# A two-layer hybrid encoder step: weight slots, token remainders and the last hidden tile around the seven-product MLP

## What is computed

```python
def _residual(x, mix, p):
    x = x + _rmsnorm(mix, p['g_post_mix'])
    f = jnp.square(jax.nn.relu(_rmsnorm(x, p['g_pre_mlp']) @ p['w_ff1'])) @ p['w_ff2']
    return x + _rmsnorm(f, p['g_post_mlp'])
```

## Time and profile before

| | |
|---|---|
| median of 3 runs | 2267.86 us (2266.67 to 2268.46) |
| the profiled execution | 2269.92 us, its span 2268.2 us |
| PE busy | 2207.9 us (97%) |
| PEld busy | 2109.3 us (93%) |
| DVE / ACT / POOL busy | 1165.3 / 1025.0 / 1022.9 us |
| chain that ended last | PE 86%, DVE 7%, ACT 3%, issue 2% |
| granted TensorE clock, mean | 0.995 |

### The profile page before, as it was taken

The page is one execution under the profiler, slowest core; times in us unless marked ns, Lnnn a source line. Parts: engine busy times, 40 slices in busy tenths (PEclk is TensorE's granted clock), DMA queues, the critical chain, the costliest instruction groups (busy, mean ns, idle before and its releaser), DMA issues.

```text
span 2268.2 us, 40754 instructions
## 1 busy us (share of the span) xinstructions
PE 2207.9 (97%) x16722; PEld 2109.3 (93%) x16722; DVE 1165.3 (51%) x2353; ACT 1025.0 (45%) x1939; POOL 1022.9 (45%) x788
## 2 busy tenths in 40 slices
PE   7999999999999999999999999999999999999997
PEld 7999988899999999999989999888999999999997
DVE  5677555535415315666576765455353261256654
ACT  4454433434555642334444544444355565324332
POOL 2423324435564463646423332244356635545642
PEclk9999999999999999999999999999999999999999
DMA  5122221122124122222321223111212422222221
GB/s 191 64 74 73 93 73 56 57 74 66 66 85 171 54 87 93 85 82 78 112 81 54 83 82 94 57 57 58 78 57 75 158 80 75 84 84 94 92 86 51
DMA packets 64569, 187.85 MB, mean 83 GB/s; under 512 B 8800, under 2 KB 17824, under 8 KB 63744
## 3 DMA queue, kind: packets, MB, share of 16 engines
q1 hardware_dynamic: 56160, 169.28, 22.2%
q10 hardware_dynamic: 8224, 15.97, 1.9%
HBM read 170.99 MB, written 10.89 MB: 80 GB/s over the span
## 4 chain that ended last, share of the span: by engine, by line
PE 86%; DVE 7%; ACT 3%; issue 2%; POOL 1%; DMA 1%; SPq 0%; DVEq 0%; ACTq 0%; POOLq 0%
PE dense L1037 39%; PE att L1037 23%; PE att L1061 4%; PE dense L1061 3%; PE att L1395 1%; PE att L1305 1%; PE dense L1117 1%; PE att L1325 1%; PE att L1162 1%; DVE h_raw L2211 1%; PE att L1353 1%; PE att L1244 1%; PE att L1240 1%; PE att L1470 1%; POOL wlo L2622 1%
## 5 line engine op out<-in xcount | busy, mean ns | idle before, releaser
L2622 POOL TENSOR_TENSOR wlo<-wraw,whi 128x1024 fp32r<-128x1024 f32 x245 | 604.4, 2481 | 491.1 <-ACT whi L1532 491.1
L1037 PE MATMUL dense<-h_hi,whi 128*128 128x280 f32 x1712 | 506.3, 296 | 4.2 <-DVE ckv L2105 1.5
L1037 PE MATMUL dense<-h_lo,whi 128*128 128x280 f32 x1712 | 499.3, 292 | 0.0
L1037 PE MATMUL dense<-h_hi,wlo 128*128 128x280 f32 x1712 | 498.1, 291 | 0.0
L1532 ACT ACTIVATE whi<-wraw 128x1024 fp32r<-128x1024 f32 x302 | 310.3, 1049 | 115.9 <-DMA wraw<-in_w 110.2
L1037 PEld LDWEIGHTS dense<-h_hi,whi 128*128 128x128 f32 x1712 | 321.9, 188 | 16.4 <-issue 9.7
L1037 PEld LDWEIGHTS dense<-h_hi,wlo 128*128 128x128 f32 x1712 | 321.4, 188 | 0.7
L1037 PEld LDWEIGHTS dense<-h_lo,whi 128*128 128x128 f32 x1712 | 321.7, 188 | 0.0
L1037 PE MATMUL att<-hid_hi,whi 128*128 128x280 f32 x704 | 209.4, 297 | 15.7 <-DVE facc L2129 6.6
L2627 POOL TENSOR_TENSOR hid_lo<-hid_raw,hid_hi 128x560 fp32r<-128x560 f32 (+1 forms) x76 | 96.2, 1271 | 257.7 <-ACT hid_hi L1557 186.4
L1037 PE MATMUL att<-hid_hi,wlo 128*128 128x280 f32 x704 | 207.1, 294 | 0.0
(11 more groups left out here) (482 smaller groups left out, 5467.4 us busy)
## 6 DMA issues: line engine op xcount, KB each, us to landing
wraw<-in_w SPq DMA_DIRECT2D x266, 512.0 KB, 3.5
wraw<-in_w SPq DMA_DIRECT2D x72, 256.0 KB, 3.5
x_spill<-x ACTq DMA_DIRECT2D x2, 2240.0 KB, 6.9
x<-x_spill ACTq DMA_DIRECT2D x2, 2240.0 KB, 12.2
k_cat<-k_rope SPq DMA_DIRECT2D x16, 212.0 KB, 3.4
x<-in_x SPq DMA_DIRECT2D x4, 560.0 KB, 7.3
out_y_out<-x SPq DMA_DIRECT2D x4, 560.0 KB, 3.1
out_c_out<-ckv SPq DMA_DIRECT2D x2, 560.0 KB, 5.5
```

The costliest lines, as they stand in the source:

```text
L1037: mm = pe.matmul(bank(u, o, hf)[0:m, :], keys, b[:, k, H[hf]], start=(k == 0 and i == 0), stop=(k == kt - 1 and i == 2))
L2622: pool.tensor_tensor(wlo[slot][:, :], wraw[slot][:, :], whi[slot][:, :].bitcast(F32), ALU.subtract).then_inc(pool_done, st.done("pool", f" ...
```

## The change

- `slots_for`: the weights of the first pair (16, 17) may not use slot `SUMS`, and "ff2 27" may not use `EDGE[3]`. By the planner's rule "ff1 even 16" goes to slot 1, "ff1 odd 16" to slot 2, "ff2 two 12" to `SUMS`, "ff2 27" to slot 2 and "ff2 28" to `EDGE[3]`.
- `w_hi`: ScalarE rounds the even tile of a pair ahead of the pair's three sums instead of behind them.
- `token_sums` on VectorE: the remainders of token sums 0, 2 and 1 come after "ff2 two" 8, 9 and 10; before, 0 and 2 came after 8 and 1 after 9.
- hidden tile 31 is activated, rounded and subtracted in two halves, far tokens first, and "ff2 two 28" runs both output tiles over the far tokens and then over the near ones.

```diff
--- before.py
+++ after.py
@@ -707,12 +707,12 @@
             def slots_for(l, u):
                 kind, n = KINDS[u]
                 if kind.startswith("ff1 ") or kind == "ff2 two":
-                    return [*BASE, *MLP] if kind == "ff2 two" and n < 12 else [*BASE, *MLP, SUMS]
+                    return [*BASE, *MLP] if (kind == "ff2 two" and n < 12) or (kind != "ff2 two" and n == STRASSEN[0]) else [*BASE, *MLP, SUMS]
                 if kind in ("out", "ff1", "ff2"):
                     if kind == "out" or (kind == "ff1" and n < 8):
                         return [*MLP, *MIX] if u in U_MIX else [*BASE, *MIX] if u in V_MLP else [*BASE] if kind == "out" else [*BASE, *MLP]
                     if kind == "ff2" and n >= 24:
-                        return [*MLP, *BASE] if u == U_MLP[0] else [*MLP, *BASE, EDGE[3]] if u in U_MLP else [*BASE]
+                        return [*MLP, *BASE] if u in U_MLP[0:2] else [*MLP, *BASE, EDGE[3]] if u in U_MLP else [*BASE]
                     return [*BASE, *MLP]
                 return [*EDGE, *BASE] if u < LAP + 2 else [*BASE]
 
@@ -1018,6 +1018,20 @@
                                     mm.then_inc(pe_done, st.done("pe", f"half {u} 0 {hf}"))
                         st.mark("pe", f"dense {u}")
                         return
+                    if (kind, n) == ("ff2 two", LAST_TWO[1]):
+                        for hf, end in ((1, " far"), (0, "")):
+                            for o in range(nout):
+                                wait_bank(u, o, hf)
+                                for k in range(kt):
+                                    if o == 0 and (hf == 1 or k == kt - 1):
+                                        for e, name in ready_names(kind, n, k):
+                                            pe.wait_ge(by_name[e], A(e, name + (end if k == kt - 1 else "")))
+                                    for i, (a, b) in enumerate(((hi_w, hi_x), (lo_w, hi_x), (hi_w, lo_x))):
+                                        mm = pe.matmul(bank(u, o, hf), a[:, o, k, :], b[:, k, H[hf]],
+                                                       start=(k == 0 and i == 0), stop=(k == kt - 1 and i == 2))
+                                mm.then_inc(pe_done, st.done("pe", f"half {u} {o} {hf}"))
+                        st.mark("pe", f"dense {u}")
+                        return
                     for o in range(nout):
                         for hf in hfs:
                             wait_bank(u, o, hf)
@@ -1519,7 +1533,12 @@
                 count = {"stored": 0}
 
                 def w_hi(u):
+                    if KINDS[u][0] == "ff1 even":
+                        return
                     if KINDS[u][0] == "ff1 sums":
+                        even = slot_of[l, u - 2]
+                        act.wait_ge(w_loaded[even], loads[l, u - 2])
+                        act.activation(whi[even][:, :], wraw[even][:, :], ACT.Copy).then_inc(act_done, st.done("act", f"w hi {u - 2}"))
                         for i, (raw, _, hi) in enumerate(sums):
                             act.wait_ge(dve_done, A("dve", f"sum {i} {u}"))
                             act.activation(hi, raw, ACT.Copy).then_inc(act_done, st.done("act", f"w hi {u} {i}"))
@@ -1535,6 +1554,14 @@
                 def strassen(u):
                     for i, parts in enumerate(((f"early early {u}", f"evac {u} 0 1"), (f"late late {u}", f"evac {u} 1 0"))):
                         n = KINDS[u][1] + i
+                        if n == ADJOINED[1] + 1:
+                            for hf, part, end in ((1, parts[0], " far"), (0, parts[1], "")):
+                                act.wait_ge(dve_done, A("dve", part))
+                                t = hid1[0][:, n % 8, H[hf]]
+                                link(act.activation(t, t, ACT.Relu))
+                                act.activation(t, t, ACT.Square).then_inc(act_done, st.done("act", f"hid {n}" + end))
+                                round_tile(hid1[2][:, n % 8, H[hf]], t, (act_done, A("act", f"hid {n}" + end)), f"hid hi {n}" + end)
+                            continue
                         for part in parts:
                             act.wait_ge(dve_done, A("dve", part))
                         t = hid1[0][:, n % 8, :]
@@ -2001,8 +2028,9 @@
                         link(dve.tensor_tensor(raw[1], raw[1], part(h_lo, 1, 1), ALU.add), "t raw 1")
                     if i == 7:
                         low(0)
+                    if i == 8:
                         low(2)
-                    if i == 8:
+                    if i == 9:
                         dve.wait_ge(pool_done, A("pool", "t raw 3"))
                         low(1)
 
@@ -2769,6 +2797,10 @@
                             pool.tensor_tensor(lo, raw, hi.bitcast(F32), ALU.subtract).then_inc(pool_done, st.done("pool", "t lo 3"))
                     elif step[0] == "strassen":
                         for n in range(KINDS[step[1]][1], KINDS[step[1]][1] + 2):
+                            if n == ADJOINED[1] + 1:
+                                for hf, end in ((1, " far"), (0, "")):
+                                    lo_tile(*(t[:, n % 8, H[hf]] for t in (hid1[1], hid1[0], hid1[2])), f"hid lo {n}" + end, f"hid hi {n}" + end)
+                                continue
                             lo_tile(hid1[1][:, n % 8, :], hid1[0][:, n % 8, :], hid1[2][:, n % 8, :], f"hid lo {n}", f"hid hi {n}")
                     elif step[0] == "masks":
                         level_masks()
```

## The result

The changed kernel takes 2295.38 us in the median (2291.71 to 2298.32) against 2268.16 us (2266.67 to 2268.51) for the kernel before on the same chip: a ratio of 1.012, 95% interval 1.0103 to 1.0138. It is 27.2 us slower where 13.6 were forecast; 2295.38 lies inside the range of 2263 to 2304, but in the place of rival (2).

A forecast was written before the change was run, and what follows sets the result against it. TensorE, busy for 97% of the span, was taken to bound the kernel; 27.7 + 3.0 - 6.9 - 0.7 - 6.3 - 3.2 = +13.6 us on the median 2267.86 gave 2281.5 us, range 2263 to 2304.

The forecast's parts named there:

- rival (2): Behind the new gaps at the steady pairs TensorE's clock falls at most: adds 15 us, 2296.5; chance 0.13.
- The steady pairs (+27.7): Pairs 18 to 28, both layers: GpSimd gets ahead of VectorE's second subtraction, each trio ends 2.31 us later, +27.7 us.
- rival (1): VectorE's subtractions at the block products keep their turn, the trio is no later: 2245 us; chance 0.12.
- The clock behind them (+3.0): Behind the twelve new TensorE gaps of some 2.4 us the clock falls at two, 1.5 us each: +3.0 us.
- The first pair (-6.9): At "ff2 two 11": new slots and moved remainders shorten TensorE's gap to 2.0 us, without slow clock: -6.9 us.
- a gap of 2.0 leaves the clock alone: At "ff2 two 11": no slow matmuls follow the shortened gap, 1.41 us gained in layer 0, 2.57 in layer 1.
- The wait for the last token remainder, put at nothing: GpSimd makes it by 919.4 to 920.0, TensorE wants it at 919.8: 0 to 0.3 us, put at nothing.
- Pair 30 (-0.7): Start of "ff1 sums 30" no longer waits (1.15 us), a later trio takes 0.8 back; net 0.35 twice, -0.7 us.
- The last tile (-6.3): Hidden tile 31 by halves at "ff2 two 28": 2.35 us gained twice and 1.60 of slow clock, -6.3 us.
- "ff2 27" (-3.2): Its weights move to slot 2, so TensorE's wait of 1.46 us and 0.16 more go, twice: -3.2 us.
- Rival (3): ScalarE reaches the even tile's rounding as late as before, so only the gains stay: 2251 us; chance 0.04.

The follow-up runs named there:

- the fillers: Changed kernel with 16 matmuls nobody reads (12 at the first pair) in each of the 14 new TensorE gaps: 2278.04 us, ratio 1.0033.
- two fillers: Changed kernel with 2 matmuls nobody reads ahead of each of the 14 waits of TensorE: 2292.36 us, ratio 1.0099.
- 4 fillers: Changed kernel with 4 matmuls nobody reads ahead of each of the 14 waits of TensorE: 2277.15 us, ratio 1.0035.

## Why the prediction was right and wrong

**The steady pairs (+27.7): right.** GpSimd does get ahead of the second subtraction, 0.44 us before it (0.4 forecast), and the trio ends 6.11 us after GpSimd's start (6.26). The steady gap grows by 2.17 us, not 2.31, so the term is 26.0. The early rounding alone shows that it is this edit, and the kernel with GpSimd behind VectorE that it is this order. The Trainium skill's page "SBUF — State Buffer", section Who interferes with whom, has it so: with two SBUF inputs the engine that issues first keeps the port. These runs agree, with 0.68 against 2.89 us for one form, told apart by one wait of GpSimd. The Trainium skill's page "Advanced Engine Details and Errata", section VectorE Performance Modes, by which a two-tensor operation and GpSimd leave each other alone, does not hold here; rival (1), which would follow from it, is out.

**The clock behind them (+3.0): the step that failed.** I took "two at 1.5" of the twelve, from the earlier trace rows, where of two gaps of 2.50 us one fell, and let a shorter gap count as safer. It fell at all twelve in the profiled execution, 12 x 1.5 = 18 us, and the fillers put the whole clock share, first pairs included, at 17.3 to 19.7 us. The price of one fall was right and their number was wrong. By the terms the change costs 29.2 us where the sum had 13.6, and 15 of the 15.6 between them are this step. Over the MLPs of all thirteen kernels, a gap of 1.77 us and more is followed by slow matmuls in 50 of 57 places (the kernel before 3 of 4, after 14 of 14, the early rounding alone 14 of 16, two fillers 9 of 11, the other kernels 10 of 12), and one of 1.74 and less in none. Gap length above that border doesn't order them: 3.40 us left the clock alone once, and 1.77 did not in four places of four. With one fall in two rows, "none to all twelve may fall" had no ground for a middle near two; the other two gaps of the kernel before, 3.37 and 3.27, had both fallen, and with them it was three of four. Rival (2) was this case, and its 2296.5 lies 1.1 us from the median; against it I had put only that "the gap is shorter than both", which the rows did not bear out, since no row lay between 1.46 and 2.50.

**The first pair (-6.9): half right.** The order of events came as worked out. Timeline of the first pair after, layer 0:

```profile
895.37 0.68 DVE L1994 TENSOR_TENSOR s_raw<-wraw 128x512 f32<-128x512 f32 x1
...
898.63 2.89 DVE L2002 TENSOR_TENSOR s_lo<-s_raw,h_hi 128x512 fp32r<-128x512 f32 x1
901.44 2.89 DVE L2002 TENSOR_TENSOR h_lo<-h_raw,h_lo 128x512 fp32r<-128x512 f32 x1
904.25 1.31 DVE L2012 TENSOR_TENSOR t_lo<-t_early,t_hi 128x1120 fp32r<-128x1120 f32 x1
...
898.19 2.78 POOL L2650 TENSOR_TENSOR wlo<-wraw,whi 128x1024 fp32r<-128x1024 f32 x1 [5.20 <-DVE wraw L1997]
...
905.98 0.49 PE L1051 MATMUL att<-hid_hi,whi 128*128 128x280 f32 x1 [1.77 <-DVE facc L2157]
```

The sums start right behind VectorE's last addition, with no wait for a load; the trio and one remainder of 1.31 us follow, and TensorE resumes 1.93 us late (2.0 forecast), in both layers. The gaps shrink by 1.60 and 1.50 (1.51 and 1.37 forecast). The step "a gap of 2.0 leaves the clock alone" failed: it fell in both layers, so of 3.98 us of slow clock only 1.0 came back, and the term is -4.1. Without the early rounding the same part gives 9.7, where 10.9 was worked out for it. The wait for the last token remainder, put at nothing, is nothing here; it is 0.3 to 1.3 us in the kernels with fillers.

**Pair 30 (-0.7): sign right.** It gave 0.59 a layer instead of 0.35. The start of "ff1 sums 30" no longer waits, and the bank of its second product does, by 0.4 us. Its trio in the kernel after, layer 0, and TensorE:

```profile
1085.73 1.91 DVE L2002 TENSOR_TENSOR s_lo<-s_raw,s_hi 128x512 fp32r<-128x512 f32 x1
1087.57 2.88 DVE L2002 TENSOR_TENSOR s_lo<-s_raw,h_hi 128x512 fp32r<-128x512 f32 x1
1090.38 1.89 DVE L2002 TENSOR_TENSOR h_lo<-h_raw,h_lo 128x512 fp32r<-128x512 f32 x1
...
1092.68 0.40 PE L1075 MATMUL att<-h_hi,whi 128*128 128x280 f32 x1 [0.40 <-DVE facc L2157]
```

All three are blocked, as forecast.

**The last tile (-6.3): right.** 2.37 us a layer and the 1.6 of slow clock went. What is left in the kernel after is the wait for tile 30 at the start of "ff2 two 28", and 0.28 us for the far half of tile 31, where TensorE's next step starts at 1104.18. TensorE's timeline, and GpSimd's near half:

```profile
1103.43 0.37 PE L1030 MATMUL att<-hid_hi,whi 128*128 128x280 f32 x1 [0.43 <-ACT hid_raw L1561]
...
1104.18 0.37 PE L1030 MATMUL att<-hid_hi,whi 128*128 128x280 f32 x1
...
1104.41 0.79 POOL L2655 TENSOR_TENSOR hid_lo<-hid_raw,hid_hi 128x280 fp32r<-128x280 f32 x1 [0.39 <-ACT hid_hi L1584]
```

The releaser named in the first row had ended by 1102.13; GpSimd's remainder of tile 30 ends at 1103.29, just before the row.

**"ff2 27" (-3.2): right**, -3.2 in the profile and -3.1 in the run with this edit alone. **Rival (3)** is out: the rounding stands at 924.29, ahead of the sums.

## What to carry to other kernels

Before an operation is moved earlier on an engine off the critical path, ask which lock or buffer it takes when it gets there: here a head start of 0.4 us for GpSimd lengthened one more subtraction on the path from 0.68 to 2.89 us, and one wait that holds GpSimd back turns a loss of 27 us into a gain of 27 (2243.69 us, ratio 0.9881). A stall of TensorE is to be priced with the clock behind it: in this kernel each new gap of some 2 us cost 2.2 us and in most places about 1.5 more. Where a stall can't be avoided, a few matmuls without use in it gave the second part back (17.3 us in the medians): four per gap were enough, two were not.

## What the runs showed of the hardware that I had not expected

- How sharp the border is for TensorE's clock: idle gaps of 1.70 to 1.74 us were followed by slow matmuls nowhere (ten places with 4 fillers), gaps of 1.91 to 1.97 in nine of eleven, and the changed kernel's two of 1.77 both. A fall is one stretch of 13 to 15 matmul steps of 0.233 us in most places, the lower of the clock's two levels, 280 columns in 0.233 us being 1.2 GHz. In the changed kernel it begins 0.3 to 1.5 us after TensorE resumes; at the gaps of 3.37 and 3.27 us in the kernel before the granted clock was at that level (0.51 and 0.50) for the last 0.5 and 1.1 us of the gap already.
- That a longer gap is not surer: 3.40 us left the clock as it was in one kernel, where 2.89 in its other layer did not. Why, no run here shows; it stays open.
- That the exclusion lengthens GpSimd as well: its piece of 128x1024 takes 2.41 us behind the trio and 2.79 ahead of it.
